# A gated convolution's input projection in Strassen's form, in a two-layer float32 trunk on one core

## What is computed

```python
def conv_mixer(h, w_in, conv_w, w_out):
    u, b_gate, c_gate, z = jnp.split(h @ w_in, 4, axis=-1)
    y = b_gate * causal_depthwise_conv(c_gate * u, conv_w)
    return (y * jax.nn.silu(z)) @ w_out

    h = rms_norm(x, norm_pre[layer])
    y = conv_mixer(h, c_w_in[o], c_conv[o], c_w_out[o])
    x = x + rms_norm(y, norm_post[layer])
```

## Time and profile before

| | |
|---|---|
| median of 3 runs | 2389.95 us (2389.32 to 2391.17) |
| profiled execution: its span, first to last instruction | 2390.5 us |
| its own time beside the span | not listed apart; the span lies within the runs |
| PE matmuls / weight loads | 11673 / 11673 |
| DVE, ACT, POOL busy | 54%, 34%, 9% |
| gated convolution: group 0 | about 1338 to 1428 us |
| groups 1 to 7 | about 1428 to 2038 us |
| output projection | about 2038 to 2213 us |
| DMA | 231 MB, mean 97 GB/s |

### The profile page before, as it was taken

One profiled execution on the slowest core, in us unless ns is written; L12 is line 12 of the kernel. 1 busy time (PEld: TensorE's weight loads), 2 busy tenths in 40 slices (PEclk: granted clock), 3 DMA queues, 4 the chain that ended last, 5 costly groups with the idle time before them and its releaser, 6 DMA issues.

```text
span 2390.5 us, 29699 instructions
## 1 busy us (share of the span) xinstructions
PE 2353.9 (98%) x11673; PEld 1942.9 (81%) x11673; DVE 1293.7 (54%) x1727; ACT 809.0 (34%) x1373; POOL 227.1 (9%) x157
## 2 busy tenths in 40 slices
PE   8999999999999999999999999999999999999998
PEld 6888888888777788888787788888888888888776
DVE  6676767654556567633566863343243334433855
ACT  5233333334344456522334421221221222322434
POOL 4000000101010010001312400000000000010400
PEclk9999999999999999999999899999999999999999
DMA  5322223233331234533222223322332232323222
GB/s 200 98 76 80 83 70 91 66 90 97 106 96 63 89 97 159 194 106 105 68 81 73 79 89 106 105 89 87 105 104 95 82 105 88 106 88 126 68 71 88
DMA packets 77980, 231.32 MB, mean 97 GB/s; under 512 B 16288, under 2 KB 19520, under 8 KB 77888
## 3 DMA queue, kind: packets, MB, share of 16 engines
q1 hardware_dynamic: 77408, 228.47, 29.7%
q10 hardware_dynamic: 480, 1.59, 0.2%
HBM read 225.29 MB, written 4.73 MB: 96 GB/s over the span
## 4 chain that ended last, share of the span: by engine, by line
PE 95%; DVE 3%; ACT 1%; issue 1%; DMA 0%; POOL 0%; DVEq 0%; SPq 0%; ACTq 0%
PE acc L909 26%; PE acc L911 25%; PE acc L910 25%; PE acc L1266 2%; PE acc L1267 2%; PE acc L1271 2%; DVE weights_lo L1403 1%; PE m L1083 1%; PE m L1091 1%; PE acc L1137 1%; PE acc L1139 1%; PE acc L1138 1%; PE m L1298 1%; PE m L1312 1%; PE m L1049 1%
## 5 line engine op out<-in xcount | busy, mean ns | idle before, releaser
L909 PE MATMUL acc<-input_hi,weights_hi 128*128 128x512 f32 (+1 forms) x2776 | 1092.0, 393 | 11.6 <-DVE weights_lo L1403 11.2
L911 PE MATMUL acc<-input_hi,weights_lo 128*128 128x512 f32 (+1 forms) x2776 | 1069.3, 385 | 0.0
L910 PE MATMUL acc<-input_lo,weights_hi 128*128 128x512 f32 (+1 forms) x2776 | 1068.4, 385 | 0.0
L1403 DVE TENSOR_TENSOR weights_lo<-weights_raw,weights_hi 128x1024 fp32r<-128x1024 f32 x400 | 529.5, 1341 | 307.8 <-ACT weights_hi L470 306.2
L909 PEld LDWEIGHTS acc<-input_hi,weights_hi 128*128 128x128 f32 x2776 | 522.7, 188 | 126.0 <-issue 14.3
L470 ACT ACTIVATE weights_hi<-weights_raw 128x1024 fp32r<-128x1024 f32 x400 | 417.4, 1059 | 611.1 <-PE acc L911 580.9
L911 PEld LDWEIGHTS acc<-input_hi,weights_lo 128*128 128x128 f32 x2776 | 522.2, 188 | 106.1
L910 PEld LDWEIGHTS acc<-input_lo,weights_hi 128*128 128x128 f32 x2776 | 522.9, 188 | 99.4 <-issue 1.9
L2125 POOL TENSOR_TENSOR small<-small 128x4 f32<-128x4 f32 (+1 forms) x19 | 25.4, 1337 | 847.7 <-DVE small L1642 371.4
L1852 DVE COPY work<-acc 128x512 f32<-128x512 f32 x48 | 31.1, 684 | 125.4 <-PE acc L911 115.1
L2049 DVE TENSOR_TENSOR work<-acc,rstd_rows 128x512 f32<-128x512 f32 x32 | 20.6, 686 | 122.6 <-PE acc L911 122.6
(11 more groups left out here) (295 smaller groups left out, 2055.6 us busy)
## 6 DMA issues: line engine op xcount, KB each, us to landing
weights_raw<-in_c_w_in SPq DMA_DIRECT2D x128, 512.0 KB, 3.7
weights_raw<-in_ab_w_in SPq DMA_DIRECT2D x126, 512.0 KB, 3.6
weights_raw<-in_m_w_kv SPq DMA_DIRECT2D x32, 512.0 KB, 3.6
weights_raw<-in_ab_w_out SPq DMA_DIRECT2D x32, 512.0 KB, 4.4
weights_raw<-in_m_w_q SPq DMA_DIRECT2D x32, 512.0 KB, 3.6
weights_raw<-in_c_w_out SPq DMA_DIRECT2D x32, 512.0 KB, 3.9
residual<-in_x SPq DMA_DIRECT2D x32, 256.0 KB, 5.8
weights_raw<-in_m_w_o SPq DMA_DIRECT2D x16, 512.0 KB, 3.5
```

The costliest lines, as they stand in the source:

```text
L909: pe.matmul(out, w_hi[:, o:o + P], hi(kt), start=kt == 0, stop=False)
L910: pe.matmul(out, w_hi[:, o:o + P], lo(kt), start=False, stop=False)
L911: last = pe.matmul(out, w_lo[:, o:o + P], hi(kt), start=False, stop=kt == last_kt)
L1403: TTO(w_lo[:, s * CW:(s + 1) * CW], raw[:, c * CW:(c + 1) * CW], w_hi[:, s * CW:(s + 1) * CW].bitcast(F32), ALU.subtract).then_inc(lo_read ...
```

## The change

Groups 1 to 7 of the input projection are computed as 28 pairs q (u, c_gate, b_gate, z of each group), each in Strassen's form in its variant with shared sums. The 2048 x 256 weight block of a pair is cut in two by input half (kt 0 to 7, 8 to 15) and output tile; the input in two by input half and token half (HT = 256 tokens). Seven products of 8 kt x 3 = 24 matmuls of 256 columns replace 4 chunks of 24 of 512. Their weights, 128 x 1024 each, are in the order of use A11, S1, S2, A12, S3, S4, A22; the S are sums formed by GpSimd from the raw blocks (r0, r1, r2, r3). The moving operands for S1, S2 and S3 are three "turned" sums of input parts, for A22 a fourth; GpSimd forms them from x during group 0 (`turned_sums`), ScalarE and VectorE split them. They lie in the place of the residual and of half of Y, so x is stored to DRAM (`x_kept`) and read back during the output projection, and Y tiles 0 to 7 go to DRAM (`y_kept`) and come back before it.

Products go to six half banks in turn. ScalarE copies the first (`p1`) and the corner C11 out of PSUM, VectorE forms v5, U2, C22, C12 and C21 (`evacuate_product`). GpSimd scales b and z by `rs` (`times_rows`). The loops over groups are written out. The weights are laid out anew on the host (`by_quarter`). The output projection takes its tiles in the order 8 to 11, 0 to 7, 12 to 15. `C_OUT1, P_OUT1` become `C_C + 16, P_C + 4`.

```diff
+S_ORDER = ("A11", "S1", "S2", "A12", "S3", "S4", "A22")
+S_BANK, S_FRESH = (0, 2, 1, 0, 1, 2, 1), 3
+S_SLOTS = 3
+TURNED_AT = {11: (0, 1), 12: (2,), 13: (3, 4), 14: (5, 6), 15: (7,)}
+def s_slot(i):
+
+    return (i + 2) % S_SLOTS
...
@@ SyncE
+                if c == 9:
+                    for k in range(KT):
+                        sp.wait_ge(*(NG(f"x{k}", 1) if k > 1 else NV(f"x{k}", 1)))
+                        sp.dma_start(dram["x_kept"][k], xt(k)).then_inc(x_kept, 16)
...
+                if n == 0:
+                    sp.wait_ge(s_used, 7 * (S_PAIRS - 1) + 2)
+                    sp.wait_ge(y_kept, 16 * 4)
+                    for k in range(KEPT_Y):
+                        sp.dma_start(xt(k), dram["y_kept"][k]).then_inc(y_back[k], 16)
+                if n == 1:
...
+                        sp.dma_start(xt(k), dram["x_kept"][k]).then_inc(x_back, 16)
@@ ScalarE
+            def s_split(i):
...
+                if i < S_SLOTS:
+                    act.wait_ge(chunk_used, C_C + 13 + s_slot(i))
+                else:
+                    act.wait_ge(s_used, i - S_SLOTS + 1)
+                s = s_slot(i)
+                act.activation(w_hi[:, s * CW:(s + 1) * CW], s_source(q, name), ACT.Copy).then_inc(s_hi, 1)
...
+            def conv_first():
                 for c in range(16):
+                    if c < 15:
+                        split(C_C + c + 1)
+                    if 9 <= c < 13:
+                        scaled(2 * (c - 9))
+                        scaled(2 * (c - 9) + 1)
+                    for kt in TURNED_AT.get(c, ()):
+                        for n in range(3):
+                            turned_high(kt, n)
+                for i in range(S_SLOTS):
+                    s_split(i)
...
+            last_input(0, 4)
+            WA.round(7)
+            last_input(4, 8)
+            z_tanh(7)
+            last_input(8, 14)
+            last_input(14, 16)
             out_phase(2, C_OUT1, P_OUT1, 4)
@@ TensorE
+            def wino_product(q, pos):
+
+                i = 7 * q + pos
+                s, out = s_slot(i), s_bank(q, pos)
+                pe.wait_ge(s_lo, i + 1)
...
+                elif pos == 3:
+                    pe.wait_ge(s_p1, q + 1)
+                else:
+                    pe.wait_ge(s_ev, evacs(q, ("U2", "v5", "C22")[pos - 4]))
+                for kt in range(8):
...
+                    o = s * CW + kt * P
+                    pe.matmul(out, w_hi[:, o:o + P], moving(pos, kt, 0), start=kt == 0 and pos < S_FRESH, stop=False,
+                              skip_group_check=True)
+                    pe.matmul(out, w_hi[:, o:o + P], moving(pos, kt, 1), start=False, stop=False, skip_group_check=True)
+                    last = pe.matmul(out, w_lo[:, o:o + P], moving(pos, kt, 0), start=False, stop=kt == 7,
+                                     skip_group_check=True)
+                last.then_inc(s_used, 1)
@@ VectorE
+            def evacuate_product(q, pos):
+
+                j, out = q % 4, s_bank(q, pos)
+                dve.wait_ge(s_used, 7 * q + pos + 1)
...
+                elif pos == 2:
+                    TTO(u2, out, p1, ALU.add).then_inc(s_ev, 1)
+                elif pos == 4:
+                    dve.wait_ge(s_ev, evacs(q, "v5"))
+                    TTO(corner_of(j, 1, 1), out, v5, ALU.add).then_inc(s_ev, 1)
...
+            def conv_step(n, step):
...
+                if step == 14:
...
+                    TTO(cu, cu, uu, ALU.mult).then_inc(*WV.did("cu"))
+                elif step == 15:
+                    dve.wait_ge(*WV.last())
+                    TTO(head2(cu), head2(cu), both_rows(rs_sq), ALU.mult).then_inc(*WV.did())
+                elif step == 16:
+                    dve.wait_ge(*WV.last())
+                    for k in range(2):
+                        o = slice(k * T, (k + 1) * T)
+                        TS(cv[:, o], cu[:, o], pcol("c_conv", (2 * n + k) * 3 + 2), None, ALU.mult).then_inc(*WV.did())
+                elif step in (17, 18):
...
+                elif step == 23:
+                    dve.wait_ge(*WG("b", n - 1))
+                    dve.wait_ge(*WV.last())
+                    TTO(cv, cv, bb, ALU.mult).then_inc(*WV.did("cb"))
...
+            def wino_group(n):
+                r = n - 1
+                WV.round(r)
+                for s in range(28):
+                    i = 28 * r + s
+                    if i:
+                        evacuate_product((i - 1) // 7, (i - 1) % 7)
+                    if i and i + 2 < S_CHUNKS:
+                        s_split(i + 2)
...
+                    finish(r, s)
+                    conv_step(n, s)
+                    if n == 7 and s >= 26:
+                        split(C_OUT1 + s - 26)
...
+            last_input(0, 4)
+            evacuate_product(S_PAIRS - 1, 6)
+            last_input(4, 8)
+            WV.round(7)
+            finish(7, 4)
+            finish(7, 5)
+            last_input(8, 16)
             out_phase(2, C_OUT1, P_OUT1, 4)
@@ GpSimd
+            def turned_sums():
+
+                pool.wait_ge(*NV("stat2", 1))
+                for kt in range(8):
...
+                    if kt > 1:
+                        pool.wait_ge(turn_lo, 3 * (kt - 1))
+                    pool.tensor_tensor(first, low[1], low[0], ALU.subtract).then_inc(turn_in, 1)
+                    pool.tensor_tensor(third, high[1], low[1], ALU.subtract).then_inc(turn_in, 1)
...
+                def first_sums(q):
+
+                    r0, r2, r3 = (s_raw[r][q % 2] for r in ("r0", "r2", "r3"))
+                    if q:
+                        pool.wait_ge(s_lo, 7 * (q - 1) + 5)
...
+                    pool.tensor_tensor(s_s3(q), r0, r2, ALU.subtract).then_inc(s_sum, 1)
...
+                    pool.tensor_tensor(r2, r2, r3, ALU.add).then_inc(s_sum, 1)
+
+                def second_sum(q):
+                    r0, r2 = (s_raw[r][q % 2] for r in ("r0", "r2"))
+                    pool.wait_ge(s_lo, 7 * q + 1)
+                    pool.wait_ge(s_sum, sums(q, "S1"))
+                    pool.tensor_tensor(r0, r2, r0, ALU.subtract).then_inc(s_sum, 1)
+
+                def fourth_sum(q):
+                    pool.wait_ge(s_lo, 7 * q + 4)
...
+                for q in range(S_PAIRS):
+                    first_sums(q)
+                    second_sum(q)
+                    if q and q % 4 in (0, 3):
+                        times_rows(q - 1)
+                    fourth_sum(q)
+                times_rows(S_PAIRS - 1)
```

More of the change, by code:

```diff
@@ L834, in _ @@
             norm(1)
-            def conv_tanh(n):
-                for j in range(2):
-                    act.wait_ge(acc_free, 2 * (P_C + 3) + j + 1 + 8 * n)
-                    act.activation(uu[:, j * T:(j + 1) * T], bb[:, j * T:(j + 1) * T], ACT.Tanh, scale=0.5)\
-                        .then_inc(*VA.did(f"z{j}"))
-            def conv_group(n, first=False, last=False):
-                for c in range(16):
-                    split(C_C + c + 1, n)
-                    if c == 0 and not first:
-                        conv_tanh(n - 1)
-                    if c == 1:
-                        VA.round(n)
-                    if last and c >= 13:
-                        split_input(1, yt, C_OUT1, 4 * (c - 13), 4 * (c - 12))
@@ new lines, in _, with last_input @@
+            for n in range(1, 8):
+                wino_group(n)
+            def last_input(first, end):
+                for k in OUT1_ORDER[first:end]:
+                    if k >= KEPT_Y:
+                        act.wait_ge(s_used, S_CHUNKS - 1)
+                        act.wait_ge(*WV("y", min(k // 2, 7)))
+                    else:
+                        act.wait_ge(s_used, S_CHUNKS)
+                        act.wait_ge(y_back[k], 16)
+                    act.activation(H_hi[:, k * T:(k + 1) * T], y_tile(k), ACT.Copy).then_inc(*YA.did(f"hi{k}"))
@@ L2105, in conv_group @@
                         dve.wait_ge(*SV.last())
-                        use_conv(n, 1)
-                    if last and c >= 13:
-                        split_input(1, yt, C_OUT1, 4 * (c - 13), 4 * (c - 12))
-            conv_group(0, first=True)
-            with dve.Fori(1, 7) as n:
-                conv_group(n)
-            conv_group(7, last=True)
-            take_conv(7, 3)
-            split_input(1, yt, C_OUT1, 12)
+                        use_conv(0, 1)
+                    for kt in TURNED_AT.get(c, ()):
+                        for n in range(3):
+                            turned_low(kt, n)
@@ new lines, in _, with last_input @@
+            for n in range(1, 8):
+                wino_group(n)
+            def last_input(first, end):
+                for k in OUT1_ORDER[first:end]:
+                    dve.wait_ge(*YA(f"hi{k}"))
+                    TTO(H_lo[:, k * T:(k + 1) * T], y_tile(k), H_hi[:, k * T:(k + 1) * T].bitcast(F32), ALU.subtract)\
+                        .then_inc(*YV.did(f"lo{k}"))
+            last_input(0, 4)
+            evacuate_product(S_PAIRS - 1, 6)
+            last_input(4, 8)
```

(1 more changed line is left out.)

315 lines of the change are left out of this document (281 added, 34 removed).

## The result

Median of 4 runs 2409.56 us (2408.70 to 2410.16), against 2390.56 us for the kernel before in the same runs: ratio 1.0078, 95% interval 1.0063 to 1.0092. The change makes this kernel slower by 0.8%. The profiled spans, 2407.8 and 2390.5 us, differ by 17.3.

A forecast was written before the change was run, and what follows sets the result against it. The prediction took PE's time to bound the gated convolution before the change, and the shared SBUF port to leave no slack after it. Terms: 2390.5 + 4.6 - 1.5 + 9.6 + 5.1 = 2408.3, forecast 2408 us, range 2360 to 2428.

The forecast's parts named there:

- The seven groups: Groups 1 to 7 of the gated convolution: 87.7 us each instead of 87.04, +4.6 us in all.
- the way in: Group 0 to the first products: turned sums delay chunks 12 to 15, product 0 and S1; +9.6 us, bounds 2 and 15.
- the way out: Output projection's start: last input tiles and pair 27's gating precede output chunk 2's split; +5.1 us, bounds 2 and 9.
- the last pair: End of the seven groups: no successor to prepare, three GpSimd sums fewer; -1.5 us.
- PE's gain: Gated convolution: 168 matmuls at 120.0 ns replace 96 at 226.7 per pair; 1.60 us for each of 28 pairs, 44.8 us.
- They don't fit together: Gated convolution: VectorE and GpSimd operations of two SBUF operands exclude each other; a low split takes 2.31 us, not 1.22.
- sum of holding times: SBUF port, per group: VectorE holds it 38.4 us and GpSimd 41.8, 80.2 of 80.64 us, no slack for waiting.
- The schedule laid out by hand: Steady group's four pairs: PE loses 0.1, 2.2 plus 1.8, 1.3 and 1.6 us in pairs 1, 2, 3, 0; 7.0 together.
- product 0 starts 3.3 us late: Way in: ScalarE's first weight split stands behind the last of eight turned tiles, which end near 1433.5; 3.3 us.
- The 1.6 us for S1: Way in, after product 0's late start: S1 is formed only then, costing 1.6 us more.
- The port costs little: Rival, 33%: GpSimd slips into VectorE's pauses, 2 us lost a group, 2371 us; 2350 at no loss in the stage.
- The clock falls too: Rival, 10%: pair 2's two waits bring half clock, half of 7 us in each group, adding 24: 2432 us.

The follow-up runs named there:

- write-only: Changed kernel with GpSimd's four weight sums per pair replaced by zero fills of the same blocks in groups 1 to 7 (computes something else): 2362.75 us.
- VectorE kernel: Changed kernel with weight sums and rstd scalings moved from GpSimd to VectorE, convolution steps, way in and output splits reordered: 2356.56 us, 0.9857 of the kernel before.
- combined kernel with tap sums at 19 and 20: Changed kernel with earlier output splits, ScalarE tap product, finish at steps 5 and 6, S3, S1 and two splits before turned tile 7, later tap sums: 2398.43 us.
- reordering that missed: Changed kernel with VectorE's finish at steps 8 and 10, tap product 17, tap sums 19 and 20, product with b 24: 2431.54 us, 1.0171 of the kernel before.

## Why the prediction was right, and where it was not

**Total.** 2408 predicted, 2409.6 measured: slower, and within 2 us. That the sum is so close is luck. The seven groups came 8.4 us below their term, the way in 7.2 above, the way out 1.5 above, the last pair 1.2 above (with the small shifts beside it in the table), and 2.2 us less half clock around the norms was no term at all. The prediction also had the groups slower than before; they are 3.8 us faster, and all of the loss lies in the way in and the way out.

**PE's gain: right.** 168 matmuls in 20.11 us, 119.7 ns each, against 120.0.

**"They don't fit together": right.** The exclusion read from the earlier trace rows sets the stage; the write-only and the VectorE kernel show it from both sides. The tap products, with one SBUF operand, take part too, as the prediction's holding times had it. The sum of holding times, 80.2 of 80.64 us, was the right warning. What it did not say is which engine pays. VectorE's queue is in order and does everything PE waits for, so the reading that counts is VectorE's time with what it is held: 79.2 of 86.5 us.

**The schedule laid out by hand: place right, size high.** Group 87.7 predicted, 86.5 measured, seven groups -3.8 us instead of +4.6. Pair by pair 0.1, 4.0, 1.3, 1.6 predicted, 0, 3.4, 0.9, 1.3 measured: every wait at the PSUM sum that was named, each between 0 and 0.6 us too long. The last pair gave 1.0 and not 1.5.

**The way in: mis-sized, +9.6 predicted, +16.8 measured.** Chunk 12 was right (2.6, measured 2.11), chunks 13 to 15 high (2.1, measured 0.83). The step that failed is "product 0 starts 3.3 us late": it was 7.5. The working let GpSimd's 256-wide blocks, 0.7 us, stand in VectorE's way; but behind the last turned tile GpSimd goes on at once with S3 and S1, 1024 wide, and the low halves of tile 7 and the split wait for both. Timelines of PE, GpSimd and VectorE after:

```profile
1438.02 0.58 PE L1621 MATMUL m<-input_hi,weights_hi 128*128 128x256 f32 x1 [7.36 <-DVE weights_lo L2339]
...
1431.38 2.35 POOL L2570 TENSOR_TENSOR weights_raw<-weights_raw 128x1024 f32<-128x1024 f32 x1
1433.87 2.34 POOL L2573 TENSOR_TENSOR weights_raw<-weights_raw,work 128x1024 f32<-128x1024 f32 x1
...
1431.90 4.59 DVE L2353 TENSOR_TENSOR turned_first<-work,turned_first 128x256 fp32r<-128x256 f32 x2 [1.06 <-ACT turned_first L996]
1436.42 0.41 DVE L2353 TENSOR_TENSOR turned_third<-work,turned_third 128x256 fp32r<-128x256 f32 x1
1436.75 1.21 DVE L2339 TENSOR_TENSOR weights_lo<-weights_raw,weights_hi 128x1024 fp32r<-128x1024 f32 x1
```

The rest was not in the sum: half clock after chunk 12 (1.7 us) and in the first product (2.4, and 0.3 in the second), and 1.6 us at pair 1's second product. The last is the one place where a transfer came late, a term the prediction took at nothing because the loads are issued a pair ahead: pair 1's is not, it waits for pair 0's fifth split. The 1.6 us for S1 did not appear.

**The way out: right place, a little low.** 5.1 predicted, 6.6 measured: the wait was 3.9 instead of 4.8, and half clock behind it, named in the prediction as a possible 3.4 and left out of the sum, took 2.7 (the 13 spacings from 2063.18 on are 5.64 us long instead of 2.95).

**The rivals.** "The port costs little" is out: its 2371 us would have needed 2 us a group, measured 6. Its 2350 us at no loss in the stage doesn't follow from its own terms, which give 2390.5 - 44.8 + 11 = 2357. "The clock falls too" was half right. After the 2.09 us wait of pair 2 the next product ran at half clock in four of seven groups, where the smallness of the waits had been my reason against it. It cost nothing there because C22's sum was late by as much: such groups show gaps of 2.09, 1.54, 0 and the others 2.09, 0.02, 1.33, and both take 86.5 us. In the combined kernel with tap sums at 19 and 20 it comes after a 2.24 us wait in four groups of seven and is hidden in part: pair 3 takes 24.5 us with it and 23.9 without. Where less else was late more was paid: 0.8 us a group with the tap product on ScalarE, and in the reordering that missed, the product behind the 3.5 us wait was 1.2 to 1.6 us too long in each of six groups. PE behind such a wait, first in the combined kernel with tap sums at 19 and 20, then in the kernel after:

```profile
1775.30:1778.70 3.40, 3.36 (x16) 3.39 (x17) 3.40 (x2) 0.98 (x2) 3.26 (x2) 0.51 0.00 0
```

```profile
1757.50:1760.90 3.40, 3.33 (x18) 3.36 (x19) 3.40 (x2) 0.00 (x0) 1.82 (x1) 0.59 0.00 0
```

**Still open.** Which order of the way in would hide the turned sums was not found; two orders gave nothing, and an earlier load of pair 1's weights was not tried. Why the half clock around the first norm lasts 10.2 us in some executions and 6.8 in others is open; that it isn't the change's work is shown by the traces alone, in which both lengths stand behind the same code.

## What to carry to other kernels

Before work is given to an engine that looks idle, ask what it costs the engine next to it while it runs. Here a GpSimd operation of two SBUF operands costs VectorE some 1.6 us of standing still, and VectorE makes the same sum in 1.22; with GpSimd's part on VectorE (and some orders changed, the output splits above all) the change is 34 us faster than the kernel before, with it on GpSimd 19 us slower. Moving single operations in a queue that is over 90% busy with its holds mostly moved the wait: the best such order gained 1 us a group, taking the holds away gained 6. And one move that put an operation right in front of its waiter cost 13 us.

## What had not been expected of the hardware

- A GpSimd fill of 128x2048 bf16, 1.80 us, does not hold VectorE's splits, which read two SBUF operands: they keep 1.22 us beside it. It does hold the tap product, which reads one: 2.10 us instead of 0.48, seven times out of seven, and the fill took 2.08 there.
- PE's clock fell to 1.2 GHz after single waits of 2.1 us in otherwise full streams, in some groups and not in others of the same kernel; after 7.4 us the next matmuls ran at half clock too (256 columns, 213 ns apart instead of 120), and after 3.9 us (512 columns, 427 instead of 227).
- VectorE with 18 more 1024-wide operations a group was busy 9 us less than without them.
